# Peer retrieval beside 47 of the expert down products, with GpSimd in the weight split and the one-hot multiply

## What is computed

```python
def _peer(h, w_q, subkeys, w_down, w_up):
    q = (hblk @ w_q).reshape(B, TB, PEER_HEADS, 2, PEER_DHALF)
    s = jnp.einsum('btphd,phnd->btphn', q, subkeys)
    v, i = lax.top_k(s, 16)
    cand = v[..., 0, :, None] + v[..., 1, None, :]        # 16 x 16 pairs
    cidx = i[..., 0, :, None] * 128 + i[..., 1, None, :]
    tv, tj = lax.top_k(cand.reshape(..., 256), 16)
    eidx = jnp.take_along_axis(cidx.reshape(..., 256), tj, axis=-1)
    w = jax.nn.softmax(tv, axis=-1)
    a = jax.nn.gelu(jnp.einsum('btd,btpkd->btpk', hblk, w_down[eidx]))
    return jnp.einsum('btpk,btpkd->btd', w * a, w_up[eidx])
```

## Time and profile before

| | |
|---|---|
| median of three executions | 3099.96 us (3099.4 to 3101.96) |
| the profiled execution | 3101.26 us, span of the trace 3099.5 us |
| PE busy | 2884.9 us, 93% |
| DVE busy | 2186.3 us, 71% |
| ACT busy | 1235.7 us, 40% |
| POOL busy | 369.4 us, 12% |
| read from device memory | 447 MB, 145 GB/s over the span |

### The profile page before, as it was taken

The page is one execution under the profiler, slowest core; times in us unless marked ns, Lnnn a source line. Parts: engine busy times, 40 slices in busy tenths (PEclk is TensorE's granted clock), DMA queues, the critical chain, the costliest instruction groups (busy, mean ns, idle before and its releaser), DMA issues. The chain is left out here.

```text
span 3099.5 us, 46116 instructions
## 1 busy us (share of the span) xinstructions
PE 2884.9 (93%) x15682; PEld 2422.1 (78%) x15682; DVE 2186.3 (71%) x4187; ACT 1235.7 (40%) x2282; POOL 369.4 (12%) x413
## 2 busy tenths in 40 slices
PE   7999999999999999999999997596479999999997
PEld 4888878567888778887859996376368999999997
DVE  2999994559898975657466664365997777777775
ACT  2323243443232332224354453153125555444554
POOL 0111116001111100100400000000473000000000
PEclk9999999999999999999999998798559999999999
DMA  5555443133545444544415556023003655666563
GB/s 233 177 176 203 170 142 102 34 109 136 197 173 194 178 162 143 185 142 148 130 49 170 180 175 216 0 69 109 1 0 96 188 185 187 186 186 188 184 189 115
DMA packets 107703, 449.94 MB, mean 145 GB/s; under 512 B 11952, under 2 KB 12592, under 8 KB 94256
## 3 DMA queue, kind: packets, MB, share of 16 engines
q1 hardware_dynamic: 93744, 347.46, 35.2%
q0 software_dynamic: 13824, 100.67, 8.6%
HBM read 447.04 MB, written 1.05 MB: 145 GB/s over the span
## 5 line engine op out<-in xcount | busy, mean ns | idle before, releaser
L178 DVE TENSOR_TENSOR weight_lo<-weight_ring,weight_hi 128x512 fp32r<-128x512 f32 x1272 | 945.5, 749 | 530.8 <-ACT weight_hi L171 515.8
L171 ACT ACTIVATE weight_hi<-weight_ring 128x512 fp32r<-128x512 f32 x1272 | 800.8, 632 | 1164.4 <-PE bank L257 1163.5
L255 PE MATMUL bank<-operand_hi,weight_hi 128*128 128x256 f32 (+1 forms) x3168 | 1039.4, 328 | 24.0 <-DVE operand_lo L592 13.0
L256 PE MATMUL bank<-operand_lo,weight_hi 128*128 128x256 f32 (+1 forms) x3168 | 1034.7, 327 | 0.0
L257 PE MATMUL bank<-operand_hi,weight_lo 128*128 128x256 f32 (+1 forms) x3168 | 1034.5, 327 | 0.0
L255 PEld LDWEIGHTS bank<-operand_hi,weight_hi 128*128 128x128 f32 x3168 | 603.7, 191 | 91.8 <-issue 21.4
L256 PEld LDWEIGHTS bank<-operand_lo,weight_hi 128*128 128x128 f32 x3168 | 603.9, 191 | 54.6
L257 PEld LDWEIGHTS bank<-operand_hi,weight_lo 128*128 128x128 f32 x3168 | 603.8, 191 | 50.8
L850 DVE SCALAR_TENSOR_TENSOR extension_ffn<-extension_ffn,silu_c 128x512 f32<-128x512 f32 x532 | 388.7, 780 | 1.7
L255 PE MATMUL bank<-hidden_hi_ffn,weight_hi 128*128 128x512 f32 (+1 forms) x704 | 256.6, 364 | 4.0 <-DVE arena L1095 4.0
L256 PE MATMUL bank<-hidden_lo_ffn,weight_hi 128*128 128x512 f32 (+1 forms) x704 | 255.3, 363 | 0.0
(11 more groups left out here) (260 smaller groups left out, 2740.1 us busy)
## 6 DMA issues: line engine op xcount, KB each, us to landing
weight_ring<-in_ffn SPq DMA_DIRECT2D x272, 512.0 KB, 3.6
weight_ring<-in_experts SPq DMA_DIRECT2D x256, 512.0 KB, 3.6
extension_ffn<-in_w_mods POOLq DMA_DIRECT2D x96, 1024.0 KB, 7.5
weight_ring<-in_w_mix SPq DMA_DIRECT2D x56, 512.0 KB, 3.6
weight_ring<-in_w_second SPq DMA_DIRECT2D x52, 512.0 KB, 4.0
extension_mixer<-in_rel_bias SPq DMA_DIRECT2D x2, 1536.0 KB, 6.8
arena<-in_x SPq DMA_DIRECT2D x1, 2048.0 KB, 9.4
arena<-in_cmp_k SPq DMA_DIRECT2D x1, 2048.0 KB, 11.8
```

What stands on the lines that cost most here:

```text
L171: nc.scalar.activation(self.hi[:, g % 2, h], self.ring[:, g % NS, h], ACT.Copy).then_inc(self.rounded, 1)
L178: self.nc.vector.tensor_tensor(self.lo[:, g % 2, h], self.ring[:, g % NS, h], self.hi[:, g % 2, h].bitcast(F32), ALU.subtract).then_inc(se ...
L255: nc.tensor.matmul(out, a_hi, b_hi, start=start and n == 0, stop=False)
L256: nc.tensor.matmul(out, a_hi, b_lo, start=False, stop=False)
```

## The change

The three stages become two, `Retrieve` and `Experts`, run with the attention's output product in one block.

- `Retrieve` has the 16 query units and then the first 47 down units (K0 = 47). The scores of a head (4 matmuls) follow its two query units. DVE does no weight subtraction in it until unit 45 of the downs (HAND_OVER): POOL does them (`subtract_beside`).
- DVE runs `best` for both blocks at once, four vectors at a time, a head as it arrives; then pairs, choosing and decoding of block 0, the pairs of block 1, the weights of block 0, and the same of block 1 with compares between its steps.
- A one-hot batch is four tokens. DVE makes both one-hots of the four in one TENSOR_TENSOR of 128x1024 (`compare`; both inputs are broadcast views of SBUF tiles). POOL multiplies the first of them, 128x512, by the weights (`weigh`), in its order half a unit after the compare and one unit of PE ahead. PE spreads four matmuls to a bank, ACT copies 512 columns.
- Downs 0 to 21 run alone, 22 to 37 with one batch after each half (block 0), 38 and 39 alone, 40 to 46 with two batches after each half, and four batches follow.
- The gelu of a down of `Retrieve` goes to one of four tiles and from there by DMA to device memory (`spill`); `Experts` reads it back, six tiles ahead, when its up unit comes.
- `Experts` has the remaining 81 downs and 128 ups: after every second pair of a new up and down one of the 47 kept ups is put in, and the last 7 kept ups end the stage. Its code and SP's loads are written out, without loops.

```diff
@@ Stream.load: written out unit by unit, for all stages
+        for g in range(lo, min(hi, self.total)):
+            if g >= NS:
+                eng.wait_ge(self.split, 2 * (g - NS + 1))
+            eng.dma_start(self.ring[:, g % NS, :], self.source[g]).then_inc(self.loaded[g % NS], 16)
@@ Units
+    def subtract_beside(self, pool, j, halves=(0, 1)):
+        g = self.g0 + j
+        for i in halves:
+            pool.wait_ge(self.rounded, 2 * g + i + 1)
+            h = slice(i * HALF, (i + 1) * HALF)
+            self.nc.gpsimd.tensor_tensor(self.lo[:, g % 2, h], self.ring[:, g % NS, h], self.hi[:, g % 2, h].bitcast(F32),
+                                         ALU.subtract).then_inc(self.split, 1)
@@
-HOTS = 8
+BATCH = 4
+NQ, K0 = 16, 47
+ALONE, PAUSE = 22, 2
+SECOND = ALONE + 16 + PAUSE
+HAND_OVER = K0 - 2
+TURN_AT, EXP_AT = [(ALONE - 1, 1), (ALONE + 14, 0)], [(ALONE - 2, 1), (ALONE + 13, 0)]
+LEFT = (P // BATCH + 4 * (K0 - SECOND), S // BATCH)
+
+def beside_down(i, half):
+    if ALONE <= i < ALONE + 16:
+        return range(2 * (i - ALONE) + half, 2 * (i - ALONE) + half + 1)
+    if SECOND <= i < K0:
+        first = P // BATCH + 4 * (i - SECOND) + 2 * half
+        return range(first, first + 2)
+    return range(0)
+
+def expert_order():
+    seq, early = [("down", K0), ("down", K0 + 1)], 0
+    for k in range(K0, NK):
+        seq.append(("up", k))
+        if k + 2 < NK:
+            seq.append(("down", k + 2))
+        if (k - K0) % 2 and early < K0:
+            seq.append(("up", early))
+            early += 1
+    return seq + [("up", k) for k in range(early, K0)]
@@ Retrieve.sync
+        for i in range(K0):
+            units.load(sp, units.g0 + NQ + NS + 2 + i, units.g0 + NQ + NS + 3 + i)
+            sp.wait_ge(self.gelu_done.sem, self.gelu_done.at(i + 1))
+            sp.dma_start(self.spill[i], self.f[i % 4]).then_inc(self.chip.spilled[i % 4], 16)
@@ Retrieve.tensor
+        def spread(b):
+            if b >= 4:
+                pe.wait_ge(self.kept.sem, self.kept.at(b - 3))
+            pe.wait_ge(self.weighted.sem, self.weighted.at(b + 1))
+            hots = self.hots(b)
+            for j in range(BATCH):
+                mm = nc.tensor.matmul(chip.bank[4 + b % 4][:, j * NK:(j + 1) * NK], hots[:, j, 0, :], hots[:, j, 1, :],
+                                      start=True, stop=True)
+            mm.then_inc(self.spread.sem, 1)
+        for i in range(K0):
+            for half in range(2):
+                units.half_chunk(pe, NQ + i, half, chip.bank[i % 2][:, 0:S], x)
+                if i == 0 and half == 0:
+                    score(PH - 1)
+                for b in beside_down(i, half):
+                    spread(b)
+                if (i, half) == TURN_AT[1]:
+                    turn(1)
+            if (i, 1) == TURN_AT[0]:
+                turn(0)
+        for b in range(*LEFT):
+            spread(b)
@@ Retrieve.gpsimd
+        def weigh(b):
+            pool.wait_ge(self.compared.sem, self.compared.at(b + 1))
+            a = self.hots(b)[:, :, 0, :]
+            w = self.columns[:, 2, BATCH * b:BATCH * (b + 1)].unsqueeze(2).to_broadcast([P, BATCH, P])
+            nc.gpsimd.tensor_tensor(a, a, w, ALU.mult).then_inc(self.weighted.sem, 1)
+        for n in range(NQ):
+            units.subtract_beside(pool, n + 2)
+        for i in range(K0):
+            for half in range(2):
+                if i + 2 < HAND_OVER:
+                    units.subtract_beside(pool, NQ + i + 2, [half])
+                for b in beside_down(i + 1, half):
+                    weigh(b)
+        for b in range(*LEFT):
+            weigh(b)
@@ Retrieve.vector
+        def compare(b):
+            dve.wait_ge(self.columns_there.sem, self.columns_there.at(b // (P // BATCH) + 1))
+            if self.last_in(b) >= 0:
+                dve.wait_ge(self.spread.sem, self.spread.at(self.last_in(b) + 1))
+            t = BATCH * b
+            nc.vector.tensor_tensor(self.hots(b), iota[:, :].unsqueeze(1).unsqueeze(1).to_broadcast([P, BATCH, 2, P]),
+                                    self.columns[:, 0:2, t:t + BATCH].rearrange("p c t -> p t c").unsqueeze(3)
+                                    .to_broadcast([P, BATCH, 2, P]), ALU.is_equal).then_inc(self.compared.sem, 1)
...
+        pairs(0)
+        for h in range(0, PH, 2):
+            choose(0, h)
+        decode(0)
+        pairs(1)
+        weights(0)
+        choose(1, 0)
+        for h in range(2, PH, 2):
+            choose(1, h)
+        decode(1)
+        for b in range(done[0], P // BATCH - 2):
+            compare(b)
+        weights(1)
+        for b in range(P // BATCH - 2, P // BATCH + 4 * (HAND_OVER - SECOND)):
+            compare(b)
@@ Experts.sync
+        for i in range(4):
+            sp.wait_ge(chip.spilled[i], 16 * ((K0 - i + 3) // 4))
+        sp.wait_ge(r.spread.sem, r.spread.at(S // BATCH))
+        for i in range(6):
+            self.reload(sp, i)
+        for j in range(len(self.seq)):
+            units.load(sp, units.g0 + NS + 2 + j, units.g0 + NS + 3 + j)
+            kind, k = self.seq[j]
+            if kind == "up" and k + 6 < K0:
+                w = self.ups.index(k)
+                sp.wait_ge(self.ffn_step.sem, self.ffn_step.at(2 * w + 1))
+                self.reload(sp, k + 6)
```

More of the change, by code:

```diff
@@ new lines, in __init__, with hots @@
+        n = S // BATCH
+        self.compared, self.weighted, self.spread, self.kept = (
+            x.take(n) for x in (chip.hot0, chip.hot1, chip.spread, chip.kept))
+        self.weight, self.columns = chip.part(0, S, NK), chip.part(E_SLOT, 3, S)
+        self.slots = chip.part(E_N, 3, SLOTS)
+        self.f = [chip.extra["early"][:, i, :] for i in range(4)]
+    def hots(self, b):
+        per = BATCH * 2 * P
+        left = b - (S // BATCH - 2)
+        at = b % 6 if left < 0 else (5, 0)[left]
+        if at < 2:
+            base = E_HOT + per * at
+        else:
+            base = (E_SC if b < P // BATCH else S * NK - 4 * per) + per * (at - 2)
+        return self.chip.part(base, BATCH, 2, P)
@@ L1930, in tensor @@
     def tensor(self, pe):
-        chip, nc, units, q, keys = self.chip, self.chip.nc, self.units, self.q, self.keys
+        chip, nc, units, r = self.chip, self.chip.nc, self.units, self.retrieve
         x = lambda kt: (self.hi[:, kt, :], self.lo[:, kt, :])
[L1933 to L1947, removed]
-    def scalar(self, act):
[L1950 to L1959, removed]
-            else:
-                nc.scalar.activation(q[:, 2 * k:2 * k + 2, :].rearrange("p a b -> p (a b)"), chip.bank[k % 2][:, :], ACT.Copy)\
-                    .then_inc(self.evicted.sem, 1)
-            units.round(act, 0, 2 * k + 3, [1])
-        act.wait_ge(self.scored.sem, self.scored.at(1))
-        for b in range(8):
-            nc.scalar.activation(self.s[:, b // 4, 4 * (b % 4):4 * (b % 4) + 4, :].rearrange("p a b -> p (a b)"),
-                                 chip.bank[b][:, :], ACT.Copy)
@@ new lines, in tensor @@
+        pe.wait_ge(r.gelu_done.sem, r.gelu_done.at(K0))
+        pe.wait_ge(r.kept.sem, r.kept.at(S // BATCH))
+        w = 0
+        for j, (kind, k) in enumerate(self.seq):
+            if kind == "down":
+                units.chunk(pe, 0, j, chip.bank[(k - K0) % 2][:, 0:S], x)
+                continue
+            pe.wait_ge(self.gated.sem, self.gated.at(w + 1))
+            for half in range(2):
+                u = units.half(pe, 0, j, half)
+                for tt in range(2):
+                    q = slice(tt * P, (tt + 1) * P)
+                    mm = product(nc, chip.bank[4 + 2 * tt + half][:, :], [((self.g_hi[:, w % 2, q], self.g_lo[:, w % 2, q]), u)],
+                                 start=(w == 0), stop=(w == NK - 1))
+                mm.then_inc(units.used, 1)
+            w += 1
@@ L2376, in build @@
                             lambda kt, g: chip.mod2[:, 3 * KT + kt:3 * KT + kt + 1], [(0, S)], add.added, spare=5)
[L2377 to L2379 removed]
+            with ExitStack() as sublayer:
+                chip.take_more(sublayer, "retrieve", early=([P, 4, S], F32))
+                retrieve = Retrieve(chip, stream, add.then, spill)
+            chip.take_more(second, "experts", act_hi=([P, 2, S], F32R), act_lo=([P, 2, S], F32R))
+            run(nc, [add, retrieve, Experts(chip, stream, retrieve)])
             stage_finish(chip, out)
```

524 lines of the change are left out of this document (257 added, 267 removed).

## The result

| | before | after |
|---|---|---|
| median (of four executions each) | 3099.91 us | 3044.95 us (3043.45 to 3047.02) |
| ratio, with its 95% interval | 1 | 0.982 (0.9804 to 0.9835) |
| span of the trace | 3099.5 us | 3045.2 us |
| PE, DVE, POOL busy | 2884.9, 2186.3, 369.4 us | 2862.2, 2171.0, 534.0 us |
| first query product to the last stage (L) | 265.4 us, no down unit done | 324.3 us, 47 down units done |

The forecast was 3044.5 us. Its two large terms were both wrong, in opposite directions: L came out 18 us shorter than the 342 forecast, the last stage 18 us longer than 589. The total is right because these cancel.

A forecast was written before the change was run, and what follows sets the result against it. PE was taken to bound nearly everywhere, DVE the retrieval, and POOL the new part from the first columns. Start 2090.1 + L 342 + last stage 589 + tail 22.9 = 3044, so 3044.5 us; forecast 3020 to 3062, range 2966 to 3085.

The forecast's parts named there:

- What bounds the kernel, and what can be won: Whole kernel: PE bounds nearly everywhere, DVE the 206.3 us retrieval; 47 down units could run beside it.
- PE to the turn, 113 us: First query product until tokens 0 to 127 are turned: 47.4 + 8 x 0.46 + 22 x 2.82 = 113 us of PE.
- DVE to the columns, 103 + 22.5 = 125.5 us: First query product to columns of tokens 0 to 127: DVE's 103 alone, plus 17 (pairs), 4 and about 1.
- From the columns on, 216.6 us: First columns to last stage, bound by POOL: 1.2 + 147 + 56 + 8 + 3 + 1.4 us.
- Multiply and subtraction at 1.37 a step: POOL from the first columns: 43 half subtractions and 64 multiplies, 107 x 1.37 = 147 us.
- Compare, +0.88 each: Compare between two POOL operations makes a step of 2.25 instead of 1.37: 56 us for 64.
- 2048-column operations, +1.94 each: Second decode beside POOL: each such DVE operation adds 1.94 us to POOL's step, four 8 us.
- the first (sharing costs less): Beside the retrieval, POOL and DVE disturb each other less: L = 263, 2966 us, halfway 3005; chance 0.20.
- The third (a slow multiply): POOL's one-hot multiply is slow from its repeated column and strided tile: at 2.6 us, +84, 3128 us; chance 0.08.
- The second (whole-instruction exclusion, by the strict rule): POOL and DVE exclude each other for whole instructions, a compare adding its full 1.22: +30, 3075 us; chance 0.20.
- The last stage, 209 x 2.82 = 589 us: Expert stage: 209 units left at PE's 2.82 us each, down or up alike, at clock 1.00: 589 us.
- At nothing: Stores and reloads on SP's queue, ACT's copies, written-out code, clock at half: all this 0 to 15 us.

The follow-up runs named there:

- the kernel with both edits: Changed kernel with the weigh put ahead of the subtractions and the iota row read from PSUM by the compare and decode's first operation: 2964.18 us, ratio 0.9562.

## Why the total was right and two terms were not

**What bounds the kernel, and what can be won.** Right. The 47 units fit beside the retrieval, and the long trough of the clock is gone (the earlier trace rows against the row above). The second stretch still has a granted clock of 0.94: it was 0.71 from 2219 to 2230 us, behind 4.0 us in which PE stood for the turn, and 0.50 from 2410.0 to 2415.4, after 5 us in which PE was busy for 2.26 and waited for the last multiplies. PE waits for POOL's multiply, 47.5 us, as forecast, and not for DVE's weights.

**PE to the turn, 113 us: wrong by 5.** The prediction took the 64 rows of the trace at L1945 for 64 matmuls and the group's 7.38 us for 0.115 each. They are 32 matmuls: a head has four (two blocks, two keys), and eight heads make 32. An fp32 matmul of this kind leaves two rows, as the earlier trace rows also show for the spreads, 256 rows for 128 tokens. A matmul is thus 0.23 us, a head's scores 0.92 and not 0.46, and a batch of four spreads the same; in place a batch takes 0.81. Eight heads add 3.7 us, and 22 down units at 2.87 instead of 2.82 another 1.1: 117.8, against the 118.0 that the PSUM pairs' kernel shows. The 2.87 is a misreading too: the prediction took down and up units as alike, and they aren't. In the kernel before, the first product of an up unit, of the next down unit and of the next up unit read:

```profile
2480.53 0.40 PE L255 MATMUL bank<-weight_hi,act_hi_experts 128*128 128x512 f32 x1
...
2483.28 0.28 PE L255 MATMUL bank<-operand_hi,weight_hi 128*128 128x256 f32 x1
...
2486.15 0.40 PE L255 MATMUL bank<-weight_hi,act_hi_experts 128*128 128x512 f32 x1
```

An up unit takes 2.75 us and a down unit 2.87; 2.82 is the mean of a stage with as many of each. In the changed kernel DVE hid the missing 5 us, since it came later. The claim that PE would need only 100 us for 25 units and 256 spreads is out by the same mistakes: 25 x 2.87 + 64 x 0.81 = 124. The two-row count could have been read from the code beside the rows, and the text ahead of the prediction has the wrong 64 as well.

**DVE to the columns, 103 + 22.5 = 125.5 us: right, 127.9.** The chosen vectors were all there 64.9 us after the first query product (61.5 forecast), and the first decode took 21.0 (19 with its waits). The pairs took 1.290 us each, near the 1.44 assumed. The part that was not priced: operations with one input wait for POOL as well. Alone the L2223 form takes 0.23:

```profile
2194.55 1.36 DVE L2223 TENSOR_SCALAR arena<-arena 128x128 uint32<-128x128 uint32 x1
```

**From the columns on, 216.6 us: 196.4 measured, with three terms off.**
- *Multiply and subtraction at 1.37 a step.* Too high, and the largest of the misses. The 1.37 came from the mixer, where by the code each operation waits for the result of the one before it. Independent ones follow each other at 1.24, and the multiply, priced as the plain form because L1252 was a little dearer than an addition, is cheaper: 0.99. So 43 x 1.24 + 64 x 0.99 = 117 instead of 147, a miss of 30. This is the term of L that was mis-sized.
- *Compare, +0.88 each.* Too low: with a compare between, a multiply's step is 1.98 instead of 0.99 and a subtraction's about 2.24 instead of 1.24, so +1.0. 64 x 0.12 = 8 us. The step of 2.25 that the prediction built for such a pair was right for a subtraction (2.24), and its -0.14 holds here too: the subtraction of 2280.17 ends at 2281.43 and the compare 1.08 behind it, 0.14 less than 1.22. The addition came out too small because the step without a compare, 1.37, was too long.
- *2048-column operations, +1.94 each.* 3.28 instead of 1.24, +2.04: right.

117 + 64 + 8 + 3 = 192, and 1.2 + 1.4 at the ends and the first compare: 195 of the 196.4. That it closes so well is in part luck. By the means of the list above, POOL's 107 operations took 39 (multiplies) and 30 (subtractions) us more than they do undisturbed, 69 in all where the terms have 75, since not every operation met a compare; and POOL stood 11.6 us for compares, which no term has. The mechanism, each engine waiting the other out, is the forecast's own. The misses of 30 and -8, less the columns 2.4 us late, make 19.6, where L is 17.7 short: two sizes were off, and for the larger one the row was badly chosen.

**The rivals.** Of the first (sharing costs less) nothing came: 1.93 us for a compare. The third (a slow multiply) was wrong by a wide margin: with a column repeated 128 times the multiply takes 1.03 us, the subtraction of two full tiles 1.26. Its sum was off as well: from 1.37 to 2.6 are 64 x 1.23 = 79 us, not 84. The second (whole-instruction exclusion, by the strict rule) differs from the forecast mainly in one price, a compare's full 1.22 us against 0.88. Measured is 1.0, between the two, and neither gives L, because both add to steps of 1.37: by the rival it would be 342 + 30 = 372 where it is 324. So the forecast's time came from sizes that cancel; that it was met says nothing for its price of a compare.

**The last stage, 209 x 2.82 = 589 us: 607.0.** The step that failed is "an up unit costs DVE 2.6 to 2.7, below 2.82". It asked whether DVE has time enough, not when it finishes. In `Experts.vector` the weigh of an up unit stands behind that same unit's subtractions, and the second of these waits for ACT, which waits for PE to leave the buffer. Up to the weigh everything is paced by PE, so the activations are ready just as PE needs them, or 0.1 later. Putting the weigh first gave 587.2, within 2 us of the forecast. The 589 was itself a little high: 81 downs at 2.87 and 128 ups at 2.75 are 584.5, and the kernel with both edits shows 585.3.

**At nothing.** The stores, the reloads, SP's waits and the code written out: right. The stores were doubled as the test. The reloads and the last stage's written-out code have no test of their own, but with 585.3 against 584.5 us that stage leaves them no more than about 1. The stores land 3.8 us after their issue and the reloads 3.5, near the 3.6 of the weights.

**What stays open.** In the kernel with the iota in PSUM the second stage takes 138.6 us where PE's own products need 124 by the prices above. Most of the 14.6 can be found in rows. In place PE takes 2.32 us for a half unit with one batch and 3.22 with two, without a wait, so its own work is 16 x 4.65 + 2 x 2.9 + 7 x 6.45 us and 4 x 0.92 for the last batches, 129 us. PE is idle for 5.5 (138.60 - 133.06), 4.8 of it for POOL's multiply. And the clock fell once, behind the 4.03 us in which PE stood for the turn:

```profile
2215.90:2222.00 6.10, 5.20 (x25) 4.91 (x24) 6.10 (x17) 1.23 (x2) 4.37 (x4) 0.50 0.24 66
```

That is about 3 us at half speed, and the three make about 137.5 of the 138.6. In the kernel with the pairs in PSUM, where PE stood 1.75 us for the turn, the granted clock stayed at 1.00. Why PE needs 0.07 us more around a batch wasn't taken apart.

## To carry to other kernels

When GpSimd is given work beside VectorE, look first at where VectorE's operands lie: one of two in PSUM cost one copy of 128 columns and was worth 61 us, more than the whole change had won. Ask of a moved step not only whether its engine has time for it but what stands ahead of it in that engine's order, since a delay of 0.15 us in 128 places hides in a busy share of 100%. And take a row's count back to the code before dividing by it, and a stage's mean unit apart by kind. With the weigh moved and the iota in PSUM the kernel takes 2964.18 us, with the pairs' inputs there too 2961.28; both are faster than the kernel before and the changed one.

## What the runs showed of the hardware

- A GpSimd TENSOR_TENSOR of 128x512 in place with one operand a column repeated takes 1.03 us (step 0.99), a subtraction of two tiles 1.26 (step 1.24); beside the compare, of two SBUF inputs, both steps are 1.0 longer. With one input of the compare in PSUM the compare takes 1.216 us in the mean, as it does (1.23) in the changed kernel at 2219.02, while POOL stands.
- One-input operations of DVE aren't spared: TENSOR_SCALAR and CAST of 128x128 uint32, 0.23 us each when not held up, take 0.96 to 1.36 beside POOL. The page of the Trainium skill named above (SBUF — State Buffer, Who interferes with whom) says that with one input DVE doesn't contend in general, but that copies, casts and tensor_scalar in two-port modes do, an exception that the prediction left out. These rows fit the exception, and MAX8 the rule; whether a two-port mode is what L2223 runs in, no run here shows.
- After PE had waited 4.0 us for the turn the granted clock was 0.50 for 6 us in the changed kernel (2219.0 to 2225.3) and in the one with the iota in PSUM (2215.9 to 2222.0); in the one with the pairs in PSUM, after 1.75 us, it was 1.00.
- An fp32 matmul of 128x128x128 leaves two rows in the trace and takes 0.23 us back to back, 0.20 in a batch of four between fp32r products.
